# A half-by-half sweep of the first gate slab, and transposes of the output inside the last units

## What is computed

```
u = rms_norm(x) @ w_in                        # q, f, i, g of 8 HGRN2 heads; q, k, v of 16/4 window heads
x = x + concat([hgrn2(...), window_attention(...)]) @ w_out
h = rms_norm(x, norm_ffn)
y = x + (silu(h @ w_gate) * (h @ w_up)) @ w_down      # D_FF = 5632
```

## Time and profile before

| | |
|---|---|
| median of 3 runs | 1394.08 us (1391.74 to 1395.69) |
| profiled execution, its own time | 1394.24 us |
| its span | 1392.0 us |
| TensorE busy | 1379.0 us |
| VectorE busy | 770.3 us |
| ScalarE busy | 533.6 us |
| GpSimd busy | 117.7 us |
| mean granted TensorE clock | 0.991 |

### The profile page before, as it was taken

The page is one execution under the profiler, slowest core; times in us unless marked ns, Lnnn a source line. Parts: engine busy times, 40 slices in busy tenths (PEclk is TensorE's granted clock), DMA queues, the critical chain, the costliest instruction groups (busy, mean ns, idle before and its releaser), DMA issues.

```text
span 1392.0 us, 23859 instructions
## 1 busy us (share of the span) xinstructions
PE 1379.0 (99%) x10396; PEld 1340.5 (96%) x10396; DVE 770.3 (55%) x978; ACT 533.6 (38%) x618; POOL 117.7 (8%) x151
## 2 busy tenths in 40 slices
PE   8999999999999999999999999999999999999998
PEld 6998999999898999999999999999999999999998
DVE  4435775478744757546455554646454554545454
ACT  5335984422334334333333333333333333333331
POOL 2010431203310062000000000000000000000000
PEclk8999999999999999999999999999999999999999
DMA  8794545544674455655555555555555555656551
GB/s 239 218 312 133 156 128 165 147 114 134 199 227 129 154 158 165 160 165 169 156 178 152 176 157 170 164 162 172 155 179 152 180 153 166 168 158 176 153 180 69
DMA packets 320739, 231.33 MB, mean 166 GB/s; under 512 B 5127, under 2 KB 292112, under 8 KB 320315
## 3 DMA queue, kind: packets, MB, share of 16 engines
q1 hardware_dynamic: 314288, 206.06, 51.4%
q0 software_dynamic: 6112, 23.59, 5.2%
q10 hardware_dynamic: 234, 0.16, 0.0%
HBM read 219.99 MB, written 14.97 MB: 169 GB/s over the span
## 4 chain that ended last, share of the span: by engine, by line
PE 97%; DVE 1%; DMA 1%; ACT 1%; issue 0%; ACTq 0%; DVEq 0%
PE acc L1528 30%; PE acc L1532 29%; PE acc L1529 29%; PE mx L1693 2%; DMA small<-const_small_dram 1%; PE acc L1542 1%; PE mx L1622 0%; PE mx L1594 0%; PE mx L1554 0%; PE mx L1480 0%; PE mx L1992 0%; PE mx L1775 0%; PE mx L1668 0%; PE acc L1545 0%; PE mx L1609 0%; PE mx L1818 0%
## 5 line engine op out<-in xcount | busy, mean ns | idle before, releaser
L1528 PE MATMUL acc<-act_h,wh 128*128 128x288 f32 x2208 | 596.6, 299 | 0.0
L1529 PE MATMUL acc<-act_l,wh 128*128 128x288 f32 x2208 | 593.7, 295 | 0.0
L634 ACT ACTIVATE wh<-raw 128x2048 fp32r<-128x2048 f32 x192 | 367.0, 1911 | 241.5 <-PE acc L1532 230.7
L987 DVE TENSOR_TENSOR wl<-raw,wh 128x2048 fp32r<-128x2048 f32 x192 | 440.2, 2293 | 1.3 <-ACT wh L634 1.2
L1528 PEld LDWEIGHTS acc<-act_h,wh 128*128 128x128 f32 x2208 | 415.6, 188 | 5.5 <-issue 4.6
L1529 PEld LDWEIGHTS acc<-act_l,wh 128*128 128x128 f32 x2208 | 414.7, 188 | 0.0
L1532 PE MATMUL acc<-act_h,wl 128*128 128x288 f32 x2208 | 324.6, 299 | 0.0
L1532 PEld LDWEIGHTS acc<-act_h,wl 128*128 128x128 f32 x2208 | 303.7, 190 | 7.4 <-issue 6.5
L1528 PE MATMUL acc<-mix_h,wh 128*128 128x288 f32 x832 | 228.7, 299 | 0.0
L1529 PE MATMUL acc<-mix_l,wh 128*128 128x288 f32 x832 | 227.9, 295 | 0.0
L1528 PEld LDWEIGHTS acc<-mix_h,wh 128*128 128x128 f32 x832 | 157.1, 189 | 2.4 <-issue 2.3
(11 more groups left out here) (271 smaller groups left out, 780.0 us busy)
## 6 DMA issues: line engine op xcount, KB each, us to landing
raw<-in_w_in_dram SPq DMA_DIRECT2D x44, 1024.0 KB, 5.9
raw<-in_w_gate_dram SPq DMA_DIRECT2D x44, 1024.0 KB, 5.7
raw<-in_w_up_dram SPq DMA_DIRECT2D x44, 1024.0 KB, 5.6
raw<-in_w_down_dram SPq DMA_DIRECT2D x44, 1024.0 KB, 5.1
raw<-in_w_out_dram SPq DMA_DIRECT2D x16, 1024.0 KB, 5.6
reg_x<-in_state_hgrn_dram POOLq DMA_DIRECT2D x16, 256.0 KB, 6.2
out_dram<-reg_x POOLq DMA_DIRECT2D x16, 256.0 KB, 3.6
bias_rows<-bias_line POOLq DMA_DIRECT2D x1, 3072.0 KB, 16.3
```

What stands on the lines that cost most here:

```text
L634: nc.scalar.activation(wh[:, s % WH, :], raw[:, s % RAW, :], ACT.Copy).then_inc(high_done, 1)
L987: nc.vector.tensor_tensor(wl[:, s % WL, :], raw[:, s % RAW, :], wh[:, s % WH, :].bitcast(F32), ALU.subtract).then_inc(low_done, 1)
L1528: mm(out, w_h[:, i, cols], a_hi[:, place(i), :], start=(i == 0), stop=False)
L1529: mm(out, w_h[:, i, cols], a_lo[:, place(i), :], start=False, stop=False)
```

## The change

Three things. (1) The first gate slab is swept in two halves of its tiles: for tiles 0 to 7 the high sweep, the low weights and the low activations, then the same for tiles 8 to 15, with the same waits for each tile; x2_ssq goes behind the slab. (2) Groups 0 to 2 of the output's transposes go behind unit 0 of the next slab in place of unit 1, and VectorE's copies of them go ahead of unit 1's add. (3) The last group is split by units: the three transposes of unit n-1 go inside unit n of the last slab, between its pairs and its low sweep; those of units 0 to 2 into mx banks 0 to 2 (384 columns), those of unit 3 behind its add, into mx bank 3 (prompt) and acc bank 0 (sampled). The copies and the stores follow in two pieces, 384 and 128 columns; there are 15 stores in place of 12.

```diff
@@ SyncE
-            for q in range(4):
-                cols = slice(512 * q, 512 * q + 512)
-                sp.wait_ge(yt_copied_a, 2 * q + 2)
-                sp.wait_ge(yt_copied_v, q + 1)
+            def store_y(cols):
                 for j in range(2):
                     sp.dma_start(y_prompt[0, P * j:P * j + P, cols], xtok[:, j, cols]).then_inc(y_out, 16)
                 sp.dma_start(y_sample.rearrange("b l d -> (b l) d")[:, cols], xtok[0:TS, 2, cols]).then_inc(y_out, 16)
-            sp.wait_ge(y_out, 16 * 12)
+
+            for q in range(3):
+                sp.wait_ge(yt_copied_a, 2 * q + 2)
+                sp.wait_ge(yt_copied_v, q + 1)
+                store_y(slice(512 * q, 512 * q + 512))
+            for n, cols in enumerate((slice(1536, 1920), slice(1920, 2048))):
+                sp.wait_ge(yt_copied_a, 8 + n)
+                sp.wait_ge(yt_copied_v, 4 + n)
+                store_y(cols)
+            sp.wait_ge(y_out, 16 * 15)
@@ ScalarE
-            for q in range(4):
+            for q in range(3):
                 y_copies(q)
+            act.wait_ge(yt_done, 4)
+            nc.scalar.activation(xtok[:, 0, 1536:1920], mx[:, 0, 0:384], ACT.Copy).then_inc(yt_copied_a, 1)
+            nc.scalar.activation(xtok[0:TS, 2, 1536:1920], mx[0:TS, 2, 0:384], ACT.Copy).then_inc(yt_copied_a, 1)
+            act.wait_ge(yt_done, 5)
+            nc.scalar.activation(xtok[:, 0:2, 1920:2048], mx[:, 3, 0:256].rearrange("p (j c) -> p j c", j=2), ACT.Copy)\
+                .then_inc(yt_copied_a, 1)
@@ VectorE, down(c)
-                    if i and c == NCH - 1:
-                        y_copy(i - 1)
                     for n in range(4):
                         m = 4 * i + n
+                        if n == 1 and i and c == NCH - 1:
+                            y_copy(i - 1)
@@ VectorE, behind ffn_walk
-            y_copy(3)
+            dve.wait_ge(yt_done, 4)
+            nc.vector.tensor_copy(xtok[:, 1, 1536:1920], mx[:, 1, 0:384]).then_inc(yt_copied_v, 1)
+            dve.wait_ge(yt_done, 5)
+            nc.vector.tensor_copy(xtok[0:TS, 2, 1920:2048], acc[0][0:TS, 0:P]).then_inc(yt_copied_v, 1)
@@ TensorE
+            def passes_by_halves(bank, s, high_sem, low_sem, place):
+                w_h = wh[:, s % WH, :].rearrange("p (k c) -> p k c", k=KD)
+                w_l = wl[:, s % WL, :].rearrange("p (k c) -> p k c", k=KD)
+                out = acc[bank][:, 0:T]
+                for half in (range(8), range(8, KD)):
+                    for i in half:
+                        pe.wait_ge(high_sem, i + 1)
+                        mm(out, w_h[:, i, :], act_h[:, place(i), :], start=(i == 0), stop=False)
+                    if half[0] == 0:
+                        pe.wait_ge(low_done, s + 1)
+                    for i in half:
+                        mm(out, w_l[:, i, :], act_h[:, place(i), :], start=False, stop=False)
+                    for i in half:
+                        pe.wait_ge(low_sem, i + 1)
+                        ins = mm(out, w_h[:, i, :], act_l[:, place(i), :], start=False, stop=(i == KD - 1))
+                ins.then_inc(unit_done, 1)
@@ TensorE, gate_up(c)
                     def between():
-                        if first:
-                            x2_ssq()
                         pe.wait_ge(low_done, s + 1)
                     if first:
-                        passes_as_they_come(bank, gu_slab(c), xgh_done, xgl_done, between, x2_place)
+                        passes_by_halves(bank, gu_slab(c), xgh_done, xgl_done, x2_place)
+                        x2_ssq()
@@ TensorE, the end
+            def y_unit(i):
+                pe.wait_ge(down_added, 16 * (NCH - 1) + 12 + i + 1)
+                if i == 0:
+                    pe.wait_ge(yt_copied_a, 6)
+                    pe.wait_ge(yt_copied_v, 3)
+                for j in range(NTT):
+                    rows = P if j < 2 else TS
+                    if i < 3:
+                        out = mx[0:rows, j, P * i:P * i + P]
+                    elif j < 2:
+                        out = mx[:, 3, P * j:P * j + P]
+                    else:
+                        out = acc[0][0:TS, 0:P]
+                    ins = nc.tensor.transpose(out, xT[:, 12 + i, P * j:P * j + rows], ident)
+                if i >= 2:
+                    ins.then_inc(yt_done, 1)
@@ TensorE, down(c)
+                        last = c == NCH - 1 and i == DN - 1
+
+                        def between():
+                            if n == 0:
+                                pe.wait_ge(low_done, s + 1)
+                            if last and n:
+                                y_unit(n - 1)
+
                         passes(n, dn_slab(c) + i, FC, slice(P * n, P * n + P), mix_h[:, half:half + FC, :],
-                               mix_l[:, half:half + FC, :],
-                               lambda: pe.wait_ge(low_done, s + 1) if n == 0 else None)
-                        if n == 1 and i and c == NCH - 1:
+                               mix_l[:, half:half + FC, :], between)
+                        if n == 0 and i and c == NCH - 1:
                             y_group(i - 1)
             ffn_walk(gate_up, down)
-            y_group(3)
+            y_unit(3)
```

## The result

| | before | changed |
|---|---|---|
| median | 1392.03 us (1390.41 to 1397.20, 20 runs) | 1390.22 us (1388.14 to 1392.56, 20 runs) |
| ratio | | 0.9982 (95% interval 0.9974 to 0.9990) |
| span of the profiled execution | 1392.0 us | 1388.0 us |
| from slab 60's first weight load to the span's end | 858.13 us | 856.10 us |

The ratio is 2.5 us (1.4 to 3.6) of 1392. The two spans lie 4.0 us apart, but 1.97 us of that lie ahead of the first place that the change touches: slab 60's first load starts at 533.87 before and at 531.90 after, though up to there both run the same program. So the table has one more line, the stretch from that load to the end. It has all of the change in it, and two profiled executions of the changed kernel give 856.10 and 856.13. (The span is given to 0.1 us, so a stretch or a tail is known to about 0.05.) It is what the experiments are read by.

What follows compares the result with a forecast made beforehand. TensorE, busy 1379.0 of 1392.0 us, was taken as the bound, so only the start and the tail could gain. -1.94 (half sweeps) + 0.5 (tail) = -1.44 us took the median 1394.08 to 1392.6, range 1390.2 to 1395.2.

Steps and rivals of the forecast that it cites:

- Part A: First gate slab, half sweeps: all 1.94 us of TensorE's waits for late tiles go, at no cost elsewhere.
- rival 2: First gate slab: last sweep still waits for act_l tiles, gain only 1.0 us, total -0.5, 1393.6 us; chance 0.13.
- rival 4: Behind the first gate slab: x2_ssq's chain becomes the bound, half sweeps gain nothing, total +0.5, 1394.6 us; chance 0.04.
- Part B, ahead of Z: Last slab: nine transposes moved ahead (0.99 us) plus a wait of 0.36 put the last low-weight sweep 1.35 us later.
- Z: Start of the last unit's low-weight sweep, 1384.40 us before the change; the tail is counted from it, 7.60 us.
- The new wait: Last slab, unit 1: TensorE's transposes of unit 0 wait 0.36 us for ScalarE's copies of group 2; bounds 0 and 0.6.
- Part B, behind Z: Tail: six store issues in a row, the last at +4.11, then 2.65 us to the end; all tail changes cost 0.5.
- Z': Forecast start of the last unit's low-weight sweep in the changed kernel, Z + 1.35 us.
- Rival 1: Kernel's end: the tail pays nothing, wait hidden and last stores landing fast, total -1.9 us, 1392.1; chance 0.15.
- Rival 3: Kernel's end: SyncE's queue of six stores backs up, slower, up to 11 us more, 1403.6; chance 0.03.

Runs made afterwards that it cites:

- the first part: Only the half sweeps of the first gate slab, x2_ssq behind it, against the kernel before: stretch 856.31 us, 1.82 less; ratio 1.0000 (0.9987 to 1.0012).

## Why the prediction was right in most of its mechanism and wrong in its call

**The call.** It gave 0.92 to "within 0.3%" and forecast 1.44 us less, which it took for less than a measurement can tell. The first step that failed is that bound: "0.3%, 4.2 us, is about what a measurement can tell" was read from three runs that spread over 3.95 us. With twenty runs on each side the interval is 0.0016 wide, 2.2 us, so 1.1 us to either side tell from no change, and 0.9982 lies clear of 1. As a number the ratio is within 0.3%, as forecast, but 1.44 us less is more than 1.1 and should have been called a small gain. (It is not far above what runs can tell: with 12 and 29 of them the first part's 1.82 us did not show.)

**The level.** 1392.6 was worked from the median of three, 1394.08. The median of twenty of the same kernel is 1392.03, so the three had come out 2 us high by chance. From that base the same sum gives 1390.6, against 1390.22 measured. The stated range (1390.2 to 1395.2) holds the result at its very edge, and for that reason: its middle was 2 us too high.

**Part A** was right term by term: 1.94 us forecast, 1.91 in the chain (8.79 to 6.88), 1.82 over the stretch when alone. No tile is waited for. VectorE ends the last low part at 538.02, and TensorE's load for it comes at 537.23 + 7 x 0.133 = 538.16, so the margin is 0.14 us where 0.1 was forecast (rival 2 falls); rstd2 did not become a bound (rival 4 falls; x2_ssq moved into the slab changes the stretch by 0.1 us at most); and TensorE stays full behind it.

**Part B, ahead of Z**: 1.35 us forecast, 1.34 measured in the chains, 1.28 and 1.30 by first loads with the same first slab on both sides (843.01 less 841.73, 843.18 less 841.88). The new wait was put at 0.36 us and is 0.34 in the row, 0.31 when taken away. Groups 0 to 2 cost nothing, as forecast.

**Part B, behind Z** is the term that was mis-sized, and the second step that failed. The order of things was right: VectorE's copy from +1.27 to +1.82 (forecast +1.39 to +1.94), first issue at +1.90 (+1.96), the sixth at +4.20 (+4.11), though its data was ready at +2.38. But "before, the last issue was 2.65 us ahead of the span's end, so the end is at Z' + 6.76" carried the old landing over: it is 1.94. Those 0.7 us turn +0.5 into -0.1. The 2.65 have in them the data of the two stores of 256 KB, which were still moving at 295 GB/s up to 1.65 us behind the last issue; in the changed kernel little is left to move 0.94 us behind it. The prediction looked at the sizes of single stores (2.3 and 2.2 us) and not at what stood ahead of them. The rule of the Trainium skill ("DMA: Bandwidth & Descriptors", section "Anatomy of one DMA") pointed the right way but gave 0.1 us of the 0.7, about what the size was worth when the sampled rows went first; the landings of 1.6 and 1.7 us here lie below its fixed part of about 2.0, which it gives for DMAs that GpSimd issues.

**Rivals.** Rival 1 (the tail pays nothing, -1.9 us) is the nearest by its number, and half its mechanism holds: the landing is at the fast end, the wait is not hidden. Rival 3 (the queue backs up) falls: the six issues start 0.43 to 0.55 us apart.

## What to carry to other kernels

A sweep that waits for tiles as they are made can lose nothing if all work on the early tiles, every pass of it, stands ahead of the first late tile; the split is right when each late tile is ready by the time that the matmuls ahead of it are done, and here it was with 24 matmuls ahead of the first late tile and not with 16 (0.86 us). At the very end count the issues of the storing queue as links of the chain: cutting the last store in two cost 0.2 us here as long as the first piece was still being issued when the second one's data was ready, and the place of one copy in VectorE's program cost 0.7 us more. With that copy ahead of the add, two pieces have a tail of 5.41 us. One group with the copy ahead was not run; in the run with one group the first issue waits for ScalarE's last copy as well (2.38 us behind Z in the changed kernel), so by these rows it could hardly have been shorter than 5.94. And an effect of 2 us in 1392 is read from a stretch of the trace that starts behind the scatter, which repeats to 0.05 us, and not from a dozen times.

## What the runs showed that I had not expected

The scatter of the times has its place and comes in steps. Over the twelve profiled executions, all of the same program up to slab 60, its first load starts anywhere from 529.29 to 536.20 us. Set beside the kernel before by VectorE's conversions, the executions differ by -1.8 to +2.4 us within the first 40 us, and by one more step between 118 and 140 us: in six of the twelve some 2.8 us are gained there, in six none. The tables of stretches of the kernel before (first fence) and of the one with the half sweeps only (second fence) show the granted clock of TensorE (the third number from the end) for that place:

```profile
115.00:145.00 30.00, 29.70 (x191) 26.96 (x190) 18.05 (x30) 19.71 (x33) 2.14 (x3) 0.89 0.39 107
```

```profile
115.00:145.00 30.00, 29.63 (x213) 27.17 (x212) 21.29 (x35) 22.96 (x43) 2.14 (x3) 1.00 0.39 106
```

It is 0.89 in the one and 1.00 in the other, and so it goes in all twelve: the six that gain have 1.00 there, the six others 0.89. What TensorE does there is the ten broadcasts of qk_broadcast, the last six of which wait for VectorE one by one, and a low-weight sweep behind them. In the chains of waits the sweep takes 4.14 us in the kernel before (first fence), twice the 2.1 of its kind, and 2.33 in the other (second fence):

```profile
123.51 4.14 PE acc L1532 x16
```

```profile
121.56 2.33 PE acc L1532 x16
```

So in one of the two TensorE runs for a while at the lower of its two levels (1.2 GHz) behind six matmuls with gaps of 0.24 to 0.45 us ahead of their weight loads. Both executions have these gaps, so they alone do not decide it, and what does was not tried. The other steps go with the clock as well. From 0 to 40 us it is 0.70 in the slowest execution (+2.4 us) and 0.91 to 0.96 in the three fastest (-1.6 to -1.8). From 250 to 280 us it is 0.83 in the first profile of the changed kernel, which gives 1.5 us back there, and 0.89 in the eleven others. Whether a kernel without the gaps at 120 us would win the 2.8 us in half its executions, more than this change, is a guess that no run here tested.
